# Seven products for eight in the head projections of a two-layer MLA and short-convolution trunk

## The chip, the cores and the metric

The kernel runs on one core of a Trainium2 chip. The metric is the device time of the program in microseconds (us). TensorE is PE in the profile (PEld is its weight load), VectorE is DVE, ScalarE is ACT, GpSimd is POOL and SyncE is SP.

## The reference

Two request groups share the weights: 512 prompt tokens and 64 sample tokens that attend to 512 cached ones. All is float32. Each of two layers computes

```
h = rmsnorm(x);  z = h @ w_in
b, c, xin, cq, ckv, kpe, ga, gb = split(z)         # 1024,1024,1024,384,256,64,1024,1024
y_a = b * causal_conv3(c * xin)
q = rmsnorm(cq) @ w_uq;  rotary parts turned       # 8 heads, 128 + 64
k = ckv_n @ w_uk;  v = ckv_n @ w_uv                # ckv_n = rmsnorm(ckv)
y_b = softmax(q k^T masked by chunks of 64) v
x += rmsnorm((sigmoid(ga) * y_a + sigmoid(gb) * y_b) @ w_o)
x += rmsnorm(relu(rmsnorm(x) @ w1)^2 @ w2)
```

The outputs are x, the new latents, rotated keys and convolution states. The gates, b, c and xin of head h are the columns 128h to 128h+127 of their parts of w_in: five blocks of 1024x128 for each head.

## The kernel before

**Layout.** Features lie on the partitions, the 576 tokens on the free axis, in two halves of 288. A float32 product is made of three fp32r matmuls (`mm3`): weight low part by x high part, high by low, high by high. So each weight block of 128x1024 (512 KB) is loaded raw into one of eight slots by SyncE, copied to a high part by ScalarE (`w_hi`) and subtracted to a low part by VectorE (`w_lo`).

**A head.** TensorE's program is written out by hand. For each of eight heads: block 0 (gate gb), the projections (an even head also makes the rotary queries of two heads and the values of two heads), block 1 (gate ga), absorbed sample queries and scores, block 2 (c), turns (transposes) of the probabilities, block 3 (xin), the attention product, block 4 (b). A block is two halves of 24 matmuls of 128x288 into a ring of four PSUM banks (`ring_free`, `ring_full`), from which VectorE scales it by the row norm `rx`. Between scores and turns stand VectorE's row maxima (L2159 to L2166), ScalarE's four exponents (L1348) and VectorE's scaling of the probabilities (L2184). `normed` releases the turns. `pv_read` says that the attention product was read from PSUM; the next head's keys wait for it.

**Loads.** SyncE loads a head's block into the slot whose block was just used (L846, after `ring_full`), five blocks ahead. In each head, after `absorbed`, it loads the small projection weights of the next one (`small_raw`). All its DMAs are on one queue, q1.

**Sums of weights.** The feed-forward's first matrix is already used in couples: 2x2 quarters with seven products instead of eight (`pair`), whose four weight sums GpSimd makes in DRAM by nine accumulating or plain DMAs each (`weight_sums`, L974 to L986, queue q0), 12 couples in each layer, after the two halves of the key's rotation (`key_rope`, L999 to L1008) of that layer.

**Start of layer 1.** SyncE waits for `row_sum`, loads the cosine and sine tables (L820, L821), then weights of head 0 (L768). ScalarE converts the second of them (L1034) in front of the key's last half.

Of the kernel before, what the change touches and what calls it, by code (L numbers as in the profile page):

```python
# [84 lines left out]
def use_hd(h, i):  # L85
    return h + (2 if SLOT_HD[i] in SLOT_P1 else 1)


def use_wo(m):
    return use_hd(HEADS, m) if m < N_HEAD else 2  # L90


def ffn_loads():
# [18 lines left out]
    uses = {SLOT_WO[m]: use_wo(m) for m in range(8)}  # L112
    use_of = {}
# [7 lines left out]
    return use_of, [uses[s] for s in range(8)]  # L121


USE_OF, SLOT_USES = ffn_loads()


# [16 lines left out]
def summed_no(L, g, p):  # L143
    return 16 * (pair_no(L, g, p) + 1)


# [3 lines left out]
R3 = HD0 + 10 * HEADS  # L150
# [14 lines left out]
def r_hd(e, i, s):  # L165
    return HD0 + 10 * e + 2 * i + s
# [130 lines left out]
class Plan:  # L297


    def __init__(self, nc, ctx):  # L300
        self.nc = nc
        self.memory()
        self.sums = nc.dram_tensor("weight_sums", (DEPTH * PAIRS, P, 4, 512), F32, kind="Internal").ap()
# [129 lines left out]
        self.left_copied = semaphore("left_copied")  # L433
        self.right_copied = semaphore("right_copied")
        self.left_added = semaphore("left_added")
        self.sum1_made = semaphore("sum1_made")
        self.sum2_made = semaphore("sum2_made")
        self.sum4_made = semaphore("sum4_made")
# [14 lines left out]
    def memory(self):  # L453
# [21 lines left out]

        self.x = put("x", [P, KC, NT])
# [7 lines left out]
        self.xh, self.xl = split("xs", [P, KC, NT])  # L484
        self.my = put("my", [P, KC, NT])
# [31 lines left out]
        self.probs = put("probs", [P, PCOLS])  # L517
        self.pth, self.ptl = split("probs_t", [P, PCOLS])
# [3 lines left out]
        turn = mark[0]  # L522
        self.cv = put("cv", [P, NT + 2])
        self.u = put("u", [P, NT + 4])
        after_head, mark[0] = mark[0], turn
        self.rope_t, self.rope_s = put("rope_t", [P, 2, NH]), put("rope_s", [P, 2, NH])
        assert mark[0] <= after_head
# [51 lines left out]
        tile, row = 4 * 4 * NH, 4 * NH  # L579
        hi_at = [small_at, small_at + 2 * tile, p1 + tile, sums]  # L580
# [123 lines left out]
def lo_made(L, n):  # L704
    return L * NBC + n + 1
# [56 lines left out]
def loads(nc, block, pl, x_in, consts, tables, blocks, small, uv, cache_t, cache_n, cache_pe, x_out):  # L762
# [3 lines left out]
    def _(sp):  # L766
# [39 lines left out]
        for L in range(DEPTH):  # L806
# [12 lines left out]
            sp.wait_ge(pl.row_sum, 2 * L + 1)  # L819
            sp.dma_start(pl.cos[:, :], tables[0]).then_inc(pl.tables_landed, 16)  # L820
# [4 lines left out]
            for p in range(HEADS // 2):  # L825
                for e in range(2):
                    for i in range(N_HEAD):
                        if i == 2:

                            sp.wait_ge(pl.absorbed, L * HEADS + p * 2 + (e + 1))  # L830
                            if e == 0:
                                odd_small(L, p)
                            elif p < HEADS // 2 - 1:
                                even_small(L, p + 1)
                            else:
                                sp.dma_start(pl.sraw[:, 0:SMV], small[L * 5 + HEADS // 2][:, 0:SMV]) \
                                    .then_inc(pl.small_landed, 16)
                        if p * 2 + e == HEADS - 1 and i == 2:
                            sp.dma_start(pl.ctraw[:, :, 0:PAST], cache_t[L]).then_inc(pl.cache_landed, 16)
                            for rows in (slice(0, ROPE), slice(ROPE, P)):  # L840
                                sp.dma_start(pl.kcraw[rows, 0:PAST], cache_pe[L]).then_inc(pl.cache_landed, 16)
                            sp.wait_ge(pl.scored, (L + 1) * HEADS * KT)
                            sp.dma_start(pl.naraw[:, :, :], cache_n[L]).then_inc(pl.nat_landed, 16)
                        sp.wait_ge(pl.ring_full, p * 20 + full(L, r_hd(e, i, 1)))

                        sp.dma_start(pl.slot(SLOT_HD[i])[2], blocks[L * NB + p * 10 + (n_head(e + 1, i))]) \  # L846
                            .then_inc(pl.slots[SLOT_HD[i]], 16)
# [23 lines left out]
            def pair_load(g, p, i):  # L871
                s = slots_pair(g, p)[i]
                to = pl.slot(s)[2]
                if i == 0:
                    slot_load(L, n_w1(g, 2 * p), s)
                elif i == 1:
                    sp.dma_start(to[:, 512:1024], blocks[L * NB + n_w1(g, 2 * p + 1)][:, 512:1024]) \
                        .then_inc(pl.slots[s], 16)
                else:
                    if i == 2:  # L880
                        sp.wait_ge(pl.sum2_made, summed_no(L, g, p))
                    else:
                        sp.wait_ge(pl.sum1_made, summed_no(L, g, p))
                        sp.wait_ge(pl.sum4_made, summed_no(L, g, p))
                    sp.dma_start(to.rearrange("p (b k) -> p b k", b=2),
                                 pl.sums[pair_no(L, g, p)][:, 2 * i - 4:2 * i - 2, :]).then_inc(pl.slots[s], 16)
# [75 lines left out]
def rotation_and_sums(nc, block, pl, blocks):  # L962
# [3 lines left out]
    def _(pool):  # L966

        def weight_sums(L, g, p):

            made, done = pl.sums[pair_no(L, g, p)], summed_no(L, g, p)  # L970
            a11, a12 = (blocks[L * NB + n_w1(g, 2 * p)][:, 512 * k:512 * (k + 1)] for k in range(2))
            a21, a22 = (blocks[L * NB + n_w1(g, 2 * p + 1)][:, 512 * k:512 * (k + 1)] for k in range(2))
            sum2, sum3, sum1, sum4 = (made[:, k, :] for k in range(4))
            pool.dma_start(sum2, a11).then_inc(pl.left_copied, 16)  # L974
            pool.dma_start(sum3, a11).then_inc(pl.left_copied, 16)
            pool.dma_start(sum1, a22).then_inc(pl.right_copied, 16)
            pool.dma_start(sum4, a12).then_inc(pl.right_copied, 16)
            pool.wait_ge(pl.left_copied, 2 * done)
            pool.dma_start(sum3, a21, accum_op=ALU.add).then_inc(pl.left_added, 16)
            pool.dma_start(sum2, a21, accum_op=ALU.add).then_inc(pl.left_added, 16)  # L980
            pool.wait_ge(pl.right_copied, 2 * done)
            pool.dma_start(sum1, a21, accum_op=ALU.add).then_inc(pl.sum1_made, 16)
            pool.wait_ge(pl.left_added, 2 * done)
            pool.dma_start(sum2, a22, accum_op=ALU.add).then_inc(pl.sum2_made, 16)
            pool.wait_ge(pl.sum2_made, done)
            pool.dma_start(sum4, sum2, accum_op=ALU.add).then_inc(pl.sum4_made, 16)  # L986
# [24 lines left out]
        for L in range(DEPTH):  # L1011
# [12 lines left out]
def scalar_engine(nc, block, pl, x_in, x_out, kv_out, kpe_out, conv_out):  # L1024
# [4 lines left out]
    def _(eng):  # L1029
# [8 lines left out]

        def head_hi(L, i):
            weight_hi(L, n_head(0, i), SLOT_HD[i], use_hd(0, i))  # L1040
# [105 lines left out]
        for L in range(DEPTH):  # L1146
# [109 lines left out]
            for p in range(HEADS // 2):  # L1256
                for e in range(2):
                    def of_head(per_head, j):
                        return L * (HEADS * per_head) + p * (2 * per_head) + (e * per_head + j + 1)
# [532 lines left out]
def vector_engine(nc, block, pl):  # L1792
# [4 lines left out]
    def _(eng):  # L1797
# [9 lines left out]
        def p1_lo(L, b):  # L1807
            weight_lo(L, b, SLOT_P1[b])
# [1559 lines left out]
```

## Time and profile before

| | |
|---|---|
| median of 3 runs | 1749.77 us (1749.56 to 1752.14) |
| the profiled execution | 1752.92 us, its span 1751.1 us |
| busy share of the span | PE 99%, PEld 98%, DVE 66%, ACT 45%, POOL 10% |
| DMA queue of SyncE, q1 | 163.82 MB |
| DMA queue of GpSimd, q0 | 56.64 MB |

The profile page divides the span into 40 slices; each digit is the busy share of a slice in tenths, and PEclk is the granted clock of TensorE in the same way. Matmuls are pipelined, so the start of one to the start of the next is their cost, not their duration. A window's row gives its length, then each engine's busy time with instruction counts, the granted clock, the mean busy share of the 16 DMA engines and their GB/s.

### The profile page before, as it was taken

The numbers are of one execution on the slowest core, as the hardware profiler recorded it, in microseconds if no ns is written. First come the engines' busy times: TensorE is split into PE (matmuls) and PEld (weight loads), VectorE is DVE, ScalarE is ACT, GpSimd is POOL, SyncE is SP. The second block draws the span as 40 slices with busy tenths as digits, with TensorE's granted clock in tenths as the row PEclk, the third lists the DMA queues.
The fourth block names the chain that finished last, engine by engine and source line by source line (L and its number), as shares of the span: only waits on it lengthen the run. The fifth ranks groups of instructions, "written<-read, shape, count | busy, mean of one in ns | idle before, by whom it ended". The sixth has DMA issues, their size and how long they took to land.

```text
span 1751.1 us, 31636 instructions
## 1 busy us (share of the span) xinstructions
PE 1736.5 (99%) x12975; PEld 1723.4 (98%) x12975; DVE 1156.4 (66%) x2232; ACT 794.3 (45%) x1541; POOL 167.9 (10%) x239
## 2 busy tenths in 40 slices
PE   9999999999999999999999999999999999999998
PEld 9999999999999999999999999999999999999997
DVE  7765555658798566657687555556577886666565
ACT  7634343335465454435366343434345545444452
POOL 0322222000000000000003222222000000000000
PEclk9999999999999999999999999999999999999999
DMA  4688878432213434333227887887513214333331
GB/s 175 174 197 178 192 176 186 106 100 76 86 52 110 131 123 133 121 116 132 74 95 157 168 159 176 148 176 155 135 62 109 74 67 164 120 116 119 126 110 55
DMA packets 83904, 224.57 MB, mean 128 GB/s; under 512 B 9776, under 2 KB 21296, under 8 KB 83760
## 3 DMA queue, kind: packets, MB, share of 16 engines
q1 hardware_dynamic: 57520, 163.82, 28.5%
q0 software_dynamic: 24960, 56.64, 19.3%
q8 instruction: 103, 1.69, 0.4%
q10 hardware_dynamic: 1280, 2.10, 0.4%
q14 instruction: 41, 0.34, 0.1%
HBM read 218.65 MB, written 60.49 MB: 159 GB/s over the span
## 4 chain that ended last, share of the span: by engine, by line
PE 97%; DMA 2%; DVE 1%; ACT 0%; SPq 0%; issue 0%; DVEq 0%
PE ring L720 20%; PE ring L722 20%; PE ring L721 20%; PE att L720 11%; PE att L722 11%; PE att L721 11%; PE att L2992 1%; DMA w_raw<-blocks_in 1%; DMA small_raw<-small_in 1%; PE att L715 1%; PE att L714 1%; PE att L727 0%; PE att L728 0%; PE att L2807 0%; PE att L3048 0%; DVE last L2761 0%
## 5 line engine op out<-in xcount | busy, mean ns | idle before, releaser
L720 PE MATMUL ring<-xs_hi,w_lo 128*128 128x288 f32 x2272 | 674.9, 297 | 0.9 <-issue 0.4
L722 PE MATMUL ring<-xs_hi,w_hi 128*128 128x288 f32 x2272 | 669.2, 295 | 0.0
L721 PE MATMUL ring<-xs_lo,w_hi 128*128 128x288 f32 x2272 | 669.0, 294 | 0.0
L720 PEld LDWEIGHTS ring<-xs_hi,w_lo 128*128 128x128 f32 x2272 | 426.7, 188 | 3.3 <-issue 0.8
L721 PEld LDWEIGHTS ring<-xs_lo,w_hi 128*128 128x128 f32 x2272 | 426.9, 188 | 1.6
L722 PEld LDWEIGHTS ring<-xs_hi,w_hi 128*128 128x128 f32 x2272 | 426.6, 188 | 0.0
L1800 DVE TENSOR_TENSOR w_lo<-w_raw,w_hi 128x1024 fp32r<-128x1024 f32 (+1 forms) x286 | 330.5, 1167 | 73.3 <-ACT w_hi L1270 60.5
L722 PE MATMUL att<-f_hi,w_hi 128*128 128x288 f32 x960 | 283.2, 295 | 0.0
L721 PE MATMUL att<-f_lo,w_hi 128*128 128x288 f32 x960 | 282.9, 295 | 0.0
L720 PE MATMUL att<-f_hi,w_lo 128*128 128x288 f32 x960 | 282.6, 294 | 0.0
L721 PEld LDWEIGHTS att<-f_lo,w_hi 128*128 128x128 f32 x960 | 180.4, 188 | 0.0
L720 PEld LDWEIGHTS att<-f_hi,w_lo 128*128 128x128 f32 x960 | 180.4, 188 | 0.0
L722 PEld LDWEIGHTS att<-f_hi,w_hi 128*128 128x128 f32 x960 | 180.4, 188 | 0.0
L1034 ACT ACTIVATE w_hi<-w_raw 128x1024 fp32r<-128x1024 f32 x106 | 109.7, 1053 | 96.9 <-DMA w_raw<-blocks_in 96.9
L2429 DVE TENSOR_TENSOR my<-att,my 128x288 f32<-128x288 f32 x160 | 73.2, 457 | 113.2 <-PE att L722 113.0
L720 PE MATMUL ring<-mix_hi,w_lo 128*128 128x288 f32 x384 | 113.4, 295 | 0.0
L722 PE MATMUL ring<-mix_hi,w_hi 128*128 128x288 f32 x384 | 113.2, 295 | 0.0
L721 PE MATMUL ring<-mix_lo,w_hi 128*128 128x288 f32 x360 | 106.2, 295 | 0.0
L1270 ACT ACTIVATE w_hi<-w_raw 128x1024 fp32r<-128x1024 f32 x80 | 84.0, 1052 | 43.4 <-DMA w_raw<-blocks_in 43.4
L1547 ACT ACTIVATE ft<-ft 128x288 f32<-128x288 f32 x96 | 42.2, 440 | 70.5 <-DVE ft L2537 35.7
L722 PEld LDWEIGHTS ring<-mix_hi,w_hi 128*128 128x128 f32 x384 | 72.3, 188 | 0.0
L720 PEld LDWEIGHTS ring<-mix_hi,w_lo 128*128 128x128 f32 x384 | 72.1, 188 | 0.0
(297 smaller groups left out, 2727.9 us busy)
## 6 DMA issues: line engine op xcount, KB each, us to landing
w_raw<-blocks_in SPq DMA_DIRECT2D x211, 512.0 KB, 4.3
weight_sums<-blocks_in POOLq DMA_DIRECT2D x192, 256.0 KB, 6.8
w_raw<-weight_sums SPq DMA_DIRECT2D x48, 512.0 KB, 3.8
w_raw<-blocks_in SPq DMA_DIRECT2D x26, 256.0 KB, 3.3
weight_sums<-weight_sums POOLq DMA_DIRECT2D x24, 256.0 KB, 6.3
small_raw<-small_in SPq DMA_DIRECT2D x16, 320.0 KB, 4.7
small_raw<-small_in SPq DMA_DIRECT2D x32, 128.0 KB, 5.9
x<-x_in SPq DMA_DIRECT2D x8, 288.0 KB, 6.8
```

The costliest lines, as they stand in the source:

```text
L714: pe.matmul(out, both, keys[1], start=False, stop=False)
L715: return pe.matmul(out, both, keys[0], start=False, stop=True)
L720: pe.matmul(out, w[1], x[0], start=first, stop=False)
L721: pe.matmul(out, w[0], x[1], start=False, stop=False)
L722: return pe.matmul(out, w[0], x[0], start=False, stop=last)
L1034: act.activation(hi, raw, ACT.Copy).then_inc(pl.weights_hi, 1)
L1270: act.activation(hi, raw, ACT.Copy).then_inc(pl.weights_hi, 1)
L1547: act.activation(ft, ft, ACT.Relu).then_inc(pl.pair_relu, 1)
L1800: return dve.tensor_tensor(out, a, hi.bitcast(F32), ALU.subtract)
L2429: dve.tensor_tensor(dst, src, dst, ALU.add).then_inc(pl.w2_free, 1)
L2992: last = pe.transpose(att[:, to:to + P], pl.probs[:, PO[t] + P * j:PO[t] + P * (j + 1)], ident)
```

## The change

Heads 2 to 6 are "mixed". Each has two couples. A couple takes two blocks of weights, A = (a11, a12) and B = (b21, b22) in quarters of 512 rows, and the two halves of tokens and of features of the normed x, and makes four results by seven products of 12 matmuls instead of eight. The first couple is c with xin (blocks 2 and 3), the second gb with ga (blocks 0 and 1); block 4 (b) stays plain. The order on TensorE in a mixed head is

```
projections, 7 products, absorbed queries and scores, block of b, turns, 3 products, attention product, 4 products
```

so there is no block in front of the projections any more. Each mixed head uses eight slots of loads instead of five (raw halves and sums), so that 55 positions in place of 40 pass the five head slots of a layer.

**Activations.** The products need the normed x itself and four mixtures of its quarters. VectorE writes x times gain times rx over x in head 0 (three rows before the row maxima, five at the end); SyncE stores it (`h_kept`) and loads it back at the end of head 1 into the low part; in head 1 VectorE makes the four mixtures (`head_mix`, 128x1152 each, two of them in front of the row maxima), ScalarE their high and VectorE their low parts, two before the attention output and two behind the merge; the normed x's parts follow in head 2. The mixtures lie where x and my lay. So each head's row of my is stored to DRAM after its merge, and at the start of head 7 SyncE stores the last row, waits for it, and loads seven rows of my and all of x (from `x_in` or `x_kept`) in front of the weights of position 55 on; in layer 1 x is first stored to `x_kept` in front of the tables.

**Sums.** GpSimd makes the sums of 22 couples per layer, 44 in all, in one run in layer 0 after the key's rotation, and only then comes to layer 1's rotation. Eight DMAs' worth of data each (one copy writes two sums), in batches: copies of sum n+1, first adds of n, second of n-1, third of n-2, after waiting for all of the batch before.

**Results.** ScalarE keeps product 0 (`snapshot`), VectorE combines the others in seven small steps per couple; since the x used is normed, the multiplications by rx fall away. In a mixed head the convolution's first tap on ScalarE comes before the exponents, VectorE's two taps between the row maxima and the probabilities, and the attention output comes after the last product and its gate. The low parts of positions at+4 to at+6 are made between the steps of the first couple.

The core of the diff:

```diff
+FIRST_MIXED, LAST_MIXED = 2, 6
...
+            def product(h, c, i):
+                n, idx = 9 * c + i, r_mixed(h, 9 * c + i)
+                eng.wait_ge(pl.ring_free, may_fill(L, idx))
+                if n % 2 == 0:
+                    eng.wait_ge(pl.weights_lo, pos_made(L, HEAD_POS[h] + n // 2))
...
+                x_of = (normed(0, 0), normed(4, 0), turned(1), turned(2), turned(3), turned(0), normed(4, 1))[i]
+                half_product(idx, half_weight(h, n), x_of, True, True).then_inc(pl.ring_full, 1)
...
+            def mixed_head(h):
+                projections(h)
+                for i in range(7):
+                    product(h, 0, i)
+                scores(h)
+                mixed_block(h)
+                turns(h)
+                for i in range(3):
+                    product(h, 1, i)
+                attended(h)
+                for i in range(3, 7):
+                    product(h, 1, i)
```

SyncE, in the loop over the heads:

```diff
+            if L > 0:
+                sp.wait_ge(pl.x_new, x_new(L - 1, "post_b", KC - 1))
+                sp.dma_start(pl.x_kept, pl.x[:, :, :]).then_inc(pl.x_spilled, 16)
             sp.dma_start(pl.cos[:, :], tables[0]).then_inc(pl.tables_landed, 16)
...
+            for h in range(HEADS):
+                if h > 0:
+                    sp.wait_ge(pl.merged, L * HEADS + h)
+                    sp.dma_start(pl.my_kept[:, h - 1, :], my_row(pl, h - 1)).then_inc(pl.my_stored, 16)
+                if h == 1:
+                    sp.wait_ge(pl.h_made, KC * (L + 1))
+                    sp.dma_start(pl.h_kept, pl.x[:, :, :]).then_inc(pl.h_stored, 16)
+                if h == HEADS - 1:
+                    sp.wait_ge(pl.my_stored, stored(L, HEADS - 2))
+                    sp.dma_start(pl.my[:, 0:KC - 1, :], pl.my_kept[:, 0:KC - 1, :]).then_inc(pl.my_landed, 16)
+                    sp.dma_start(pl.x[:, :, :], x_in if L == 0 else pl.x_kept).then_inc(pl.x_back, 16)
+                for j in range(HEAD_POS[h + 1] - HEAD_POS[h]):
...
+                    elif is_mixed(h):
+                        sp.wait_ge(pl.ring_full, full(L, r_mixed(h, (1, 3, 5, 8, 9, 11, 13, 15)[j])))
+                    else:
+                        sp.wait_ge(pl.ring_full, full(L, r_hd(h, j, 1)))
+                    pos_load(HEAD_POS[h] + j + N_HEAD)
```

GpSimd, and VectorE's order in head 1 and in a mixed head:

```diff
+            for n in range(n_sums + 2):
+                if n < n_sums:
+                    pool.wait_ge(pl.sums_copied, 48 * (n + 1))
+                if 1 <= n <= n_sums:
+                    pool.wait_ge(pl.sums_first, 32 * n)
+                if 2 <= n <= n_sums + 1:
+                    pool.wait_ge(pl.sums_second, 16 * (n - 1))
+                if n >= 3:
+                    pool.wait_ge(pl.sums_third, 16 * (n - 2))
+                if n + 1 < n_sums:
+                    sums_copy(n + 1)
+                if n < n_sums:
+                    sums_add_first(n)
+                if 1 <= n <= n_sums:
+                    sums_add_second(n - 1)
+                if n >= 2:
+                    sums_add_third(n - 2)
...
-            for g in range(FIRST_PAIR, GROUPS):
-                for p in range(2):
-                    weight_sums(L, g, p)
+            if L == 0:
+                all_sums()
...
+                elif h == FIRST_MIXED - 1:
+                    head_mix(0)
+                    head_mix(1)
+
+                row_maxima(h)
...
+                pos_lo(L, at + 6)
+                lower_right(0, pl.v2[:, :])
+                upper_right(0, pl.cv[:, cols(1)])
+                conv_second_half()
+
+                row_maxima(h)
+                absorbed_lo(h, pl.rest)
+                conv_taps(h)
+                probabilities(h)
```

## Rows read from the trace of the kernel before

**Rows 1.** Page: busy time, and granted clock in 40 slices.
```profile
PE 1736.5 (99%) x12975; PEld 1723.4 (98%) x12975; DVE 1156.4 (66%) x2232; ACT 794.3 (45%) x1541; POOL 167.9 (10%) x239
...
PEclk9999999999999999999999999999999999999999
```

**Rows 2.** TensorE's waits: us in total, times, longest.
```profile
PE att L720 <- DVE ckv_lo L1800: 2.4, 1, 2.4
...
PE att L720 <- DVE probs_t_lo L1800: 1.1, 1, 1.1
```

**Rows 3.** Windows by stage, head 2 of layer 0; DMA share last but one.
```profile
148.04:157.08 9.04, 9.04 (x68) 8.77 (x67) 5.29 (x12) 6.86 (x16) 2.77 (x4) 1.00 0.92 212
157.08:163.44 6.36, 6.36 (x51) 6.36 (x49) 4.02 (x8) 2.34 (x5) 0.83 (x1) 1.00 0.70 97
163.44:167.07 3.63, 3.63 (x27) 3.41 (x26) 1.73 (x3) 1.80 (x3) 0.26 (x1) 1.00 0.93 128
...
180.88:182.74 1.86, 1.86 (x15) 1.73 (x13) 0.64 (x3) 1.02 (x3) 0.00 (x0) 1.00 1.12 184
```

**Rows 4.** Timeline of VectorE in the same head: start, us, instruction.
```profile
151.24 0.46 DVE L2125 TENSOR_TENSOR rope_t<-att,cos 128x288 f32<-128x288 f32 x1 [5.71 <-ACT rope_s L1108]
...
152.10 0.46 DVE L2128 TENSOR_TENSOR rope_t<-rope_t,rope_s 128x288 f32<-128x288 f32 x1
...
165.80 1.23 DVE L1800 TENSOR_TENSOR w_lo<-w_raw,w_hi 128x1024 fp32r<-128x1024 f32 x1 [1.70 <-ACT w_hi L1270]
...
169.38 0.29 DVE L2174 TENSOR_TENSOR q_abs_lo<-att,u 128x128 fp32r<-128x128 f32 x1
...
171.94 1.27 DVE L2184 TENSOR_SCALAR probs<-probs,ri 128x128 f32<-128x128 f32 x4
...
188.15 0.19 DVE L2235 TENSOR_SCALAR gate_sample<-gb 128x64 f32<-128x64 f32 x1
188.25 0.68 DVE L2237 SCALAR_TENSOR_TENSOR my<-gb,att 128x512 f32<-128x512 f32 x1
...
189.89 0.69 DVE L2092 TENSOR_TENSOR my<-my,ga 128x512 f32<-128x512 f32 x1
```

**Rows 5.** DMA view: queue's packets, MB, share; issues with us to landing.
```profile
q1 hardware_dynamic: 57520, 163.82, 28.5%
...
w_raw<-blocks_in SPq DMA_DIRECT2D x26, 256.0 KB, 3.3
...
x_out<-x ACTq DMA_DIRECT2D x2, 288.0 KB, 2.3
```

**Rows 6.** Loads of w_raw, from 100 to 320 us and from 340 to 440 us.
```profile
DMA to landing us min/median/max: 3.5/5.6/7.6
...
DMA to landing us min/median/max: 3.4/3.7/5.3
```

**Rows 7.** Queues in windows 59:66, 277:300 (two), 613:700, 1189.5:1216 us.
```profile
q0 software_dynamic: 304, 1.00, 47.3%
...
q0 software_dynamic: 1040, 2.36, 58.2%
q1 hardware_dynamic: 457, 1.62, 23.7%
...
q1 hardware_dynamic: 3302, 11.00, 38.6%
...
q0 software_dynamic: 1040, 2.36, 60.4%
```

**Rows 8.** Chain that ended last, at the start of layer 1.
```profile
908.91 8.76 DMA w_raw<-blocks_in
...
917.70 1.06 ACT w_hi L1034
```

**Rows 9.** Timeline of GpSimd: first sum of layer 0, rotation of layer 1.
```profile
59.66 0.71 POOL L974 DMA_DIRECT2D weight_sums<-blocks_in  x1
...
913.76 0.79 POOL L999 TENSOR_TENSOR rope_t<-kpe,cos 128x288 f32<-128x288 f32 x1 [592.87 <-DMA sin<-tables_in]
```

More of the change, by code:

```diff
@@ L110, in ffn_loads @@
     order += [("w2", g, j) for g, j in W2_LAST]
-    uses = {SLOT_WO[m]: use_wo(m) for m in range(8)}
-    use_of = {}
+    uses, use_of = [int(s in SLOT_P1) for s in range(8)], {}
+    for q in range(POSITIONS + N_HEAD):
+        two = any(is_mixed(h) and HEAD_POS[h] + 2 <= q < HEAD_POS[h] + 7 for h in range(HEADS))
+        uses[pos_slot(q)] += 2 if two else 1
+        use_of["pos", q] = uses[pos_slot(q)]
+    for m in range(N_HEAD, 8):
+        uses[SLOT_WO[m]] += 1
+        use_of["wo", m] = uses[SLOT_WO[m]]
     for block in order:
@@ L824, in _ @@
                 slot_load(L, n_head(0, i), SLOT_HD[i])
[L825 to L847, printed above, removed]
@@ L966, in _ @@
     def _(pool):
[L968 to L986, printed above, removed]
@@ new lines, in rotary_lo @@
+            def rotary_lo(h):
+                for half in range(2):
+                    cs = cols(half)
+                    eng.wait_ge(pl.rope_hi, h + (L * 8 + half + 1))
+                    for rows, other, both in ((slice(0, ROPE), slice(ROPE, P), pl.pe0),
+                                              (slice(ROPE, P), slice(0, ROPE), pl.pe1)):
+                        ins = minus(both[other, cs], pl.rope_t[rows, half, :], both[rows, cs])
+                    ins.then_inc(pl.rope_lo, 1)
@@ new lines, in keys, with values @@
+            def keys(h):
+                eng.wait_ge(pl.pv_read, of_head(h, 1, 0))
+                for c in range(CC):
+                    last = mm3(pe, att[:, 1024:1536], small_w(SK, c), rows_of(ckv, ALL, c, slice(0, NP_)),
+                               c == 0, c == CC - 1)
+                last.then_inc(pl.projected, 1)
+            def values(two):
+                tiles = value_tiles(pl, two)
+                for kt in range(2):
+                    at = P * (2 * two + kt)
+                    for c in range(CC):
+                        last = mm3(pe, tiles[:, kt, :, :], rows_of(ckv, ALL, c, slice(at, at + P)),
+                                   rows_of(small, ALL, slice(SV + 2 * P * c, SV + 2 * P * (c + 1))),
+                                   c == 0, c == CC - 1)
+                last.then_inc(pl.projected, 1)
@@ new lines, in turns @@
+            def turns(h):
+                eng.wait_ge(pl.normed, of_head(h, 4, KT - 1))
+                eng.wait_ge(pl.abs_lo, of_head(h, 1, 0))
+                for j, at in enumerate((1536, 0, 512, 768)):
+                    for t in range(j, KT):
+                        to = at + P * (t - j)
+                        last = pe.transpose(att[:, to:to + P], pl.probs[:, PO[t] + P * j:PO[t] + P * (j + 1)], ident)
+                    if j != 2:
+                        last.then_inc(pl.turned, 1)
@@ new lines, in half_weight, with half_product @@
+            def half_weight(h, n):
+                hi, lo, _ = pl.half_slot(pos_slot(HEAD_POS[h] + n // 2), n % 2)
+                return hi, lo
+            def half_product(idx, weight, x_of, first, last):
+                for k in range(4):
+                    w = slice(k * P, (k + 1) * P)
+                    ins = mm3(pe, pl.ring[:, bank(L, idx), 0:NH], (weight[0][:, w], weight[1][:, w]), x_of(k),
+                              first and k == 0, last and k == 3)
+                return ins
```

1141 lines of the change are left out of this document (758 added, 383 removed).

## Prediction

> **What bounds the kernel now.** I read the busy row and the forty slices first [rows 1]: TensorE is busy 99% of the span, at full clock in every slice, while VectorE stands at 66% and ScalarE at 45%. Then TensorE's waits [rows 2]: 2.4 us for ckv_lo in layer 1, 1.1 for a low part of the turned probabilities, and no longer one in the heads. So every matmul left out gains its pitch, and every wait on TensorE's way is new time. The stages of head 2 in layer 0 [rows 3] give all lengths: projections of an even head 9.04 us, a block of 48 matmuls 6.36 (0.1325 each), absorbed queries and scores 3.63, attention product 1.86. The last column but one matters as much: the DMA engines stand at 0.70 to 1.12 there, because GpSimd's queue makes the weight sums.
>
> **The gain.** Before, a head has five blocks, 240 matmuls. After, a mixed head has two couples of seven products of 12 and one block: 168 + 48 = 216. 24 x 0.1325 = 3.18 us, in 5 heads of 2 layers: **31.8 us** off. All matmuls kept have their old shapes.
>
> **Layer-wide costs, each on the path.** Times below count from T, the start of the head in question on TensorE.
> (a) Head 1. VectorE now makes two mixes of 128x1152 before its row maxima. A 128x1024 difference takes 1.23 us [rows 4], so two take some 2.6 with the wait between them. Before, VectorE finishes w_lo at 167.03 and the scores end at 167.07; from there maxima, exponents and probabilities last until 173.21, and the block that covers them until 167.07 + 6.36 = 173.43 [rows 3, 4]: no slack. Cost 2.6 us per layer.
> (b) Head 2's start. It has no block 0 in front any more (6.36 us of cover). At the end of head 2 the attention output began at 188.15 and the merge ended at 190.58 [rows 4], with the next head at 182.74 + 6.36 = 189.10 [rows 3]. In head 1 one low weight of 1.2 goes away in front of it and two low parts of mixes come, 1.3 each: merge at T+2.9; two more behind it: T+5.5. The first rotary sum takes 1.3 us [rows 4], T+6.8, and TensorE wants it at T+5.2 (18 matmuls of queries 2.4; of the 4.3 us left of 9.04 for keys and values, by columns 1.4 each for keys and half the values). Then a normed low part stands before the low keys (0.8 us more), another before product 1 (0.4), and VectorE reaches the row maxima 0.8 late. About 3.7 us per layer.
> (c) Heads 3 to 6. The keys want pv_read, which now comes after the last product: with 0.3 until the last product can be read, 0.46 combination, 0.69 and 0.2 gate and 0.78 attention output (widths as in [rows 4]) TensorE has it at T+2.5 against T+2.4. About 0.2 each, 0.8 per layer.
> (d) The slot at+6 is loaded when product 3 is done, 4.8 us before the scores. Two halves of 256 KB land 3.3 us after the second issue [rows 5], at -0.6; ScalarE 1.05, VectorE 1.2 [rows 4, 8], then lower right 0.95, upper right 0.45, convolution input 0.5: +3.6, and the scores end at +3.63. Borderline: 0 to 0.5, I take 0.2 a head, 1.0 per layer.
> (e) Head 7. SyncE waits for the merge of head 6 (T+3.3), stores its row (288 KB, 2.3 us by the nearest store [rows 5]), and issues at T+6 the rows kept, 2.06 MB, and x, 2.36 MB. Behind them on the same queue comes the weight for position 55, 0.52 MB, which ScalarE converts before the absorbed queries and VectorE before the row maxima. The queue needs 28.5% of 1751 us for 163.8 MB [rows 5], 3.05 us per MB: 4.94 MB land at T+6.3+15.1+1.5 = T+22.9; +1.05+1.2 = T+25.1. The scores end at T+20.1 (6.36+3.78+6.36+3.63). The row maxima start 5.0 us late, per layer. Bounds: 0, if a load doesn't wait for larger ones in front of it, and 20, below.
> [...] The queue's own row gives 328 GB/s over the span, so I keep 3.05 us per MB.
> (f) Layer 1 only: x, 2.36 MB, is stored in front of the tables and of three weights of head 0. The second of these landed 8.76 us after 908.91; ScalarE, which has key and latent work behind it, started it at 917.70; this ended in the 2.4 us wait [rows 2, 8]. With 2.36 x 3.05 = 7.2 us more in front, the wait grows by 7.1. Nothing covers it; bounds 0 and 14 (a queue shared with the sums).
> Sum: layer 0 13.1, layer 1 20.2 us. Other new loads, the extra ScalarE copies and the 1.68 us of taps lie in idle time: the two taps, some 1.7 us by the 128x512 line, fit the time from 169.67 to 171.94 in which VectorE waited for exponents [rows 4].
>
> **Costs of a full DMA in layer 0.** GpSimd now makes all 44 sums in one run from about 60 us on [rows 9], batch behind batch, instead of 12 in each layer. So all heads and the feed-forward of layer 0 run beside them. Before, the same contention made a weight load land in 5.6 us (median, up to 7.6) against 3.7 in the quiet stretch [rows 6], without a wait on TensorE. Now (d) has no slack: 1.8 us in each of five heads, 9 us. The slot at+10, loaded 8.2 us before the head's end, delays lower right and with it pv_read: 1.2 us in four heads, 5 us. (e) has 15.1 us of transfer that shares its engines; at the factor that 5.6 against 3.7 gives on 1.6 us of transfer (2.2, less for pauses between batches: 1.6) it is 24, +9 us. Sum **23 us**; bounds 0 and 45. The feed-forward's loads land several us before VectorE's turn, so I charge nothing there; if that cover were gone, each pair would cost a us or two.
>
> **Does GpSimd finish in time?** Its next duty is layer 1's key rotation, at 913.76 before [rows 9]. A sum's nine DMAs took 58.2% of 23 us, 13.4 us of all engines, the four copies 3.3 of it (47.3% of 7 us) [rows 7]; now four copies and four adds, about 11. With 3 us for issue and receipt between batches and SyncE's queue taking 0.24 to 0.39 of the engines [rows 7], a batch takes 17 to 21 us; 45 of them end between 825 and 1005. The share of 1.12 in [rows 3] says that the queues overlap a little, so I take 19.3: 930. The need moves to 913.8 + 7 (f) + 20 (layer 0) = 941. Just in time: charge 0, with the overrun as a rival.
>
> **Sum.** -31.8 + 13.1 + 20.2 + 23 = +24.5 us on the profiled execution, whose own time is 1752.92 (span 1751.1); that one stands 3.15 us above the median of the runs. So 1749.8 + 24.5 = **1774 us**.
>
> **Rivals.**
> Rival 1, GpSimd is late. In layer 1 a sum needed 60.4% of 26.5 us, 16 us instead of 13.4 [rows 7]; if the sums of layer 1 are as dear when made early, batches take 22 us after the first 22 and the run ends near 1000. Layer 1's rotation then waits 40 to 60 us, TensorE with it: about 1820. For it: those rows. Against: before, latency filled much of each chain. It begins where a batch takes over 19.6 us.
> Rival 2, the queues share without harm: layer 0 costs what layer 1 does, no 23 us. -31.8 + 33.3 = +1.5, 1751. For it: sums before cost TensorE nothing. Against: the slack that made this so is what the change uses up.
> Rival 3, the other side: loads behind a large transfer aren't held up, since sixteen engines take both in turn. Then (e) and (f) fall away and contention too: -31.8 + 16.2 = -15.6, 1734. It decides if position 55 lands by T+18. Against it: the weight of 8.76 us in [rows 8], which had only 1.6 MB in front.
> [...]
>
> **Chances and range.** Forecast 0.40, rival 1 0.25, rival 2 0.15, rival 3 0.20. Half of rival 3 lies under 1733 and the far part of rival 1 over 1830, so the range is 1733 to 1830; the forecast's own is 1760 to 1795. A change under 0.2% (3.5 us) can't be told from none. Faster: rival 3 and a part of rival 2, 0.22; same 0.07; slower 0.71.
>
> **What would show it.** Right: TensorE waits before turns in heads 1 and 7 of both layers, about 2.6 and 5 us (14 in layer 0); a wait of some 9 us near layer 1's start with a weight load behind it; landings of 6 us or more in layer 0 up to its end, under 4 in layer 1's heads; 12735 matmuls. Wrong: position 55 lands within 12 us of T+6; GpSimd's DMAs end before 800 (they were cheap in batches) or after 950 (rival 1), then with a wait on kpe in layer 1; or TensorE's waits sum to under 30 us. A lower granted clock behind the longer waits would add to all of this.

## The result and the profile after

The changed kernel takes 1911.44 us (median of 4 runs, 1904.33 to 1916.63) against 1749.66 (1749.02 to 1752.14): a ratio of 1.0919, 95% interval 1.0881 to 1.0957. The forecast was 1774 us, its range 1733 to 1830. The page of its profiled execution, in answer to [rows 1] (busy time, then three of the lines in 40 slices):

```profile
span 1907.8 us, 31819 instructions
...
PE 1730.6 (91%) x12735; PEld 1711.7 (90%) x12735; DVE 1254.1 (66%) x2370; ACT 855.2 (45%) x1617; POOL 245.8 (13%) x331
...
PE   9989899989999999999940099999999999999998
...
PEclk9989999999999999999975599999999999999999
DMA  5698889897777988997876433433361222433331
```

The 240 matmuls less are there and TensorE's busy time is 6 us shorter, but it stands still in slices 21 to 23. Its waits, in answer to [rows 2]:

```profile
PE att L797 <- DVE rope_t L2369: 109.3, 3, 106.0
PE att L3456 <- DVE probs L2409: 36.4, 9, 12.2
PE att L797 <- DVE ckv_lo L2051: 12.2, 2, 11.6
```

One wait of 106.0 us is in layer 1's start; the second row is turns in the heads that wait for VectorE's probabilities. The chain of what ended last runs through GpSimd's queue: "issue" (time in which an engine stood and the profile shows nothing that it waited for) has 30.0% of the span there and DMAs of weight_sums 13.2%. The next rows are the timeline of GpSimd, to be read beside [rows 9], at its last sum, and that of TensorE behind it (start, duration; in brackets the idle time before and what ended it):

```profile
1085.42 0.81 POOL L1129 DMA_DIRECT2D weight_sums<-weight_sums  x1 [5.09 <-DMA weight_sums<-weight_sums]
1085.97 1.08 POOL L1164 TENSOR_TENSOR rope_t<-kpe,cos 128x288 f32<-128x288 f32 x1
...
1093.64 0.61 PE L797 MATMUL att<-cqn_hi,small_lo 128*128 128x288 f32 x1 [106.04 <-DVE rope_t L2369]
```

The rotation of layer 1 starts right behind the issue of the last sum, at 1085.97 instead of 913.76 [rows 9]. The first rotary sum of head 0 on VectorE stands behind the key in program order, so the wait shows under its name. Where the time went, by the start of the turns of head 0 and head 7 in each layer (taken at their first weight load):

| stretch | before | after | difference |
|---|---|---|---|
| start to turns of head 0, layer 0 | 83.6 | 83.7 | +0.1 |
| to turns of head 7, layer 0 | 311.3 | 349.0 | +37.7 |
| to turns of head 0, layer 1 | 555.0 | 681.7 | +126.7 |
| to turns of head 7, layer 1 | 312.7 | 305.0 | -7.7 |
| to the end | 488.5 | 488.4 | -0.1 |

The rows of the windows (length, busy times, granted clock, DMA share, GB/s) say what stood beside each stretch:

```profile
60.00:440.00 380.00, 341.31 (x2390) 333.37 (x2390) 256.53 (x509) 167.97 (x310) 85.48 (x116) 0.94 0.86 211
440.00:900.00 460.00, 456.60 (x3444) 456.02 (x3443) 311.07 (x573) 214.70 (x402) 100.83 (x136) 1.00 0.83 192
...
972.00:1083.00 111.00, 6.53 (x30) 5.78 (x30) 6.12 (x10) 6.47 (x15) 26.61 (x35) 0.53 0.61 97
1130.00:1450.00 320.00, 313.92 (x2293) 307.47 (x2292) 242.16 (x487) 157.29 (x292) 0.00 (x0) 0.99 0.44 143
```

Heads with sums beside them (first row) lose 39 of 380 us and some of the clock. Heads without (last row) run nearly full and are faster than before. And the 37.7 us of layer 0 are not even part of the end: the rotation waited for GpSimd, whose run of sums began at the same 60 us as before, so without the 37.7 us TensorE would only have stood longer. On the path stand 172.2 us of rotation later, less 7.7 between rotation and first turns (28.4 for 36.1 us; I take it that TensorE had by then done all that needs no key), less 7.7 in layer 1's heads: 156.8, the difference of the two spans (156.7).

Why was GpSimd late? Its 44 sums took from 60 to 1086, 22.4 us each from the last add of the first (122.1) to that of the last (1085.4). One batch, while the feed-forward ran:

```profile
613.65 0.77 POOL L1116 DMA_DIRECT2D weight_sums<-blocks_in  x1 [5.12 <-DMA weight_sums<-weight_sums]
614.40 0.57 POOL L1117 DMA_DIRECT2D weight_sums<-blocks_in  x1
614.94 0.55 POOL L1118 DMA_DIRECT2D weight_sums<-blocks_in  x1
615.47 0.93 POOL L1122 DMA_DIRECT2D weight_sums<-blocks_in  x1
623.13 0.84 POOL L1123 DMA_DIRECT2D weight_sums<-blocks_in  x1 [6.74 <-issue]
623.68 1.13 POOL L1126 DMA_DIRECT2D weight_sums<-weight_sums  x1
632.06 0.81 POOL L1129 DMA_DIRECT2D weight_sums<-weight_sums  x1 [7.26 <-issue]
637.96 0.76 POOL L1116 DMA_DIRECT2D weight_sums<-blocks_in  x1 [5.09 <-DMA weight_sums<-weight_sums]
```

The program waits only in front of L1116. Yet GpSimd stands before L1123 and L1129, each time 7 us, and the trace has no semaphore for it ("issue"). The view of GpSimd's waits counts them over the whole span:

```profile
POOL weight_sums L1123 <- issue: 273.3, 42, 14.5
POOL weight_sums L1129 <- issue: 261.2, 42, 8.8
```

535 us of standing that the prediction's batch did not have.

### The profile page after: what moved, and what is told of

Read it like the earlier page. It is cut to its first block, busy times and chain, and to the rows that moved or that the text cites. A ratio compares the mean times of both kernels' runs of the same rounds, so it can differ in the third digit from the quotient of the medians.

```text
span 1907.8 us, 31819 instructions
## 1 busy us (share of the span) xinstructions
PE 1730.6 (91%) x12735; PEld 1711.7 (90%) x12735; DVE 1254.1 (66%) x2370; ACT 855.2 (45%) x1617; POOL 245.8 (13%) x331
## 3 DMA queue, kind: packets, MB, share of 16 engines
q1 hardware_dynamic: 76288, 204.32, 32.8%
q0 software_dynamic: 38720, 92.29, 27.4%
q10 hardware_dynamic: 1280, 2.10, 0.3%
## 4 chain that ended last, share of the span: by engine, by line
PE 40%; issue 30%; DMA 16%; POOL 10%; DVE 3%; ACT 1%; SPq 0%; POOLq 0%; DVEq 0%; ACTq 0%
DMA weight_sums<-weight_sums 13%; PE ring L797 8%; PE ring L799 8%; PE ring L798 8%; PE att L797 5%; PE att L799 5%; PE att L798 5%; POOL weight_sums L1122 2%; POOL weight_sums L1126 2%; POOL weight_sums L1123 2%; POOL weight_sums L1116 2%; POOL weight_sums L1117 1%; DMA w_raw<-blocks_in 1%; POOL weight_sums L1118 1%; DMA weight_sums<-blocks_in 1%
## 5 line engine op out<-in xcount | busy, mean ns | idle before, releaser
L797 PE MATMUL ring<-xs_hi,w_lo 128*128 128x288 f32 x1872 | 561.0, 300 | 1.6 <-ACT kpe L1341 0.5
L798 PE MATMUL ring<-xs_lo,w_hi 128*128 128x288 f32 x1872 | 555.0, 296 | 0.0
L799 PE MATMUL ring<-xs_hi,w_hi 128*128 128x288 f32 x1872 | 554.5, 296 | 0.0
L2051 DVE TENSOR_TENSOR w_lo<-w_raw,w_hi 128x1024 fp32r<-128x1024 f32 (+1 forms) x316 | 367.7, 1171 | 119.7 <-ACT w_hi L1206 82.9
L797 PEld LDWEIGHTS ring<-xs_hi,w_lo 128*128 128x128 f32 x1872 | 355.9, 190 | 4.4 <-issue 1.3
L798 PEld LDWEIGHTS ring<-xs_lo,w_hi 128*128 128x128 f32 x1872 | 355.7, 190 | 1.6
L799 PEld LDWEIGHTS ring<-xs_hi,w_hi 128*128 128x128 f32 x1872 | 355.2, 190 | 0.0
L1206 ACT ACTIVATE w_hi<-w_raw 128x1024 fp32r<-128x1024 f32 x118 | 124.4, 1056 | 168.9 <-DMA w_raw<-weight_sums 85.8
L1198 ACT ACTIVATE w_hi<-w_raw 128x1024 fp32r<-128x1024 f32 x98 | 102.3, 1056 | 109.8 <-DMA w_raw<-blocks_in 109.8
L797 PE MATMUL att<-cqn_hi,small_lo 128*128 128x288 f32 x144 | 43.5, 302 | 106.3 <-DVE rope_t L2369 106.0
L797 PEld LDWEIGHTS att<-cqn_hi,small_lo 128*128 128x128 f32 x144 | 28.0, 195 | 106.7 <-DVE rope_t L2369 106.2
```

Of the source, the lines that this page charges most:

```text
L797: pe.matmul(out, w[1], x[0], start=first, stop=False)
L798: pe.matmul(out, w[0], x[1], start=False, stop=False)
L799: return pe.matmul(out, w[0], x[0], start=False, stop=last)
L1198: act.activation(hi, raw, ACT.Copy).then_inc(pl.weights_hi, 1)
L1206: act.activation(hi, raw, ACT.Copy).then_inc(pl.weights_hi, 1)
L2051: return dve.tensor_tensor(out, a, hi.bitcast(F32), ALU.subtract)
```

## The experiments

Times of before, measured beside the runs: 1750.25 us for runs 1, 2, 3 and 5, 1749.55 for 6, 7, 9 and 10, 1750.63 for 4, 8 and 11. L0 and L1 below are the stretches from turns of head 0 to turns of head 7 in the two layers.

**1. Sums of each layer in that layer.**

```diff
-            if L == 0:
-                all_sums()
+            layer_sums(L)     # 22 sums, same batches
```

> All 44 sums are still made in batches, but the 22 of layer 1 only after layer 1's key rotation. Theory 'GpSimd is late' (the rotation queued behind 44 batches costs the 106 us stop of TensorE in layer 1 and a few us of half clock behind it): the stop falls away, some 1911 - 108 = 1803 us if layer 1's heads stay as fast as they are, and up to 45 us more, 1848, if sums beside the heads cost in layer 1 what they cost in layer 0 (turns of head 0 to turns of head 7: 349 us against 305). Rival (the stop has another cause, the stored x or the tables): still a stop of 100 us, 1900 or more.

1832.71 us (1829.39 to 1851.78), ratio 1.0494 (1.044 to 1.0549). The stop is gone: the rotation starts at 950.35, and TensorE's longest wait for a rotary sum is 2.2 us. L0 is 343.0 and L1 351.7, where it was 305.0. So the late rotation is the cause of the stop, and sums beside mixed heads cost layer 1 some 47 us too.

**2 and 3. GpSimd's DMA scratch and its use.** In the first, one number of the program's set-up, the size of its DMA scratch; in the second, one issue. I expected 1820 to 1870 us of both and 19 to 22 us a sum. "Descriptor space", here and in run 4, is only my name for the scratch: no trace shows what it holds, and that GpSimd stands because it is full is my inference.

```diff
-    nc = bacc.Bacc(..., dynamic_dma_scratch_size=1024)
+    nc = bacc.Bacc(..., dynamic_dma_scratch_size=1280)
```

> [...] Rival (the DMA engines themselves are the limit, at a share of 0.83): batches and time unchanged, 1905 to 1915.

```diff
-            pool.dma_start(pl.sums[n][:, 2, :], b[:, 512:1024], accum_op=ALU.add)...
-            pool.dma_start(pl.sums[n][:, 1, :], b[:, 0:512], accum_op=ALU.add)...
+            pool.dma_start(pl.sums[n][:, 1:3, :], b.rearrange("p (k c) -> p k c", k=2), accum_op=ALU.add)...
```

> The two first adds of a sum, 256 KB each, are one DMA of 512 KB: the same bytes, one issue less. [...] Rival (bytes through the engines): batch 23.3 us, time 1905 to 1915.

1823.88 us (1.0424, 1.0408 to 1.0439) and 1810.46 us (1.0325, 1.0286 to 1.0364). The sums end at 930.8 and 927.5 us, 19.1 and 19.0 us each; the rotations, at 987.96 and 978.03, wait for the sine table and no longer for GpSimd. (Run 3 came out faster than the 1820 that I expected at the least.) The timeline of GpSimd with 1280 bytes:

```profile
605.13 0.76 POOL L1116 DMA_DIRECT2D weight_sums<-blocks_in  x1 [10.43 <-DMA weight_sums<-weight_sums]
605.88 0.57 POOL L1117 DMA_DIRECT2D weight_sums<-blocks_in  x1
606.41 0.55 POOL L1118 DMA_DIRECT2D weight_sums<-blocks_in  x1
606.94 0.91 POOL L1122 DMA_DIRECT2D weight_sums<-blocks_in  x1
607.49 1.21 POOL L1123 DMA_DIRECT2D weight_sums<-blocks_in  x1
614.93 0.81 POOL L1126 DMA_DIRECT2D weight_sums<-weight_sums  x1 [6.23 <-issue]
615.46 1.14 POOL L1129 DMA_DIRECT2D weight_sums<-weight_sums  x1
```

One stop instead of two, and one DMA later (in front of L1126 instead of L1123), as I had expected; the bytes of both queues are unchanged (92.29 and 204.32 MB). The stop that is left is not small: in all sums together GpSimd still stands 245 us in run 2 and 286 in run 3, against 535. And the time is not 1774: L0 is 367.9 and 360.4, longer than the 349.0 of the change, and the stretch between the layers' heads is 573.8 and 569.2 where it was 555.0 before. I put this down to the faster queue: from 84 to 433 us the DMA engines' share is 0.93 and 0.89, against 0.88 in the change.

**4. Half the space.** Same line, 512.

> The changed kernel with 512 bytes of descriptor scratch instead of 1024, nothing else. Theory 'descriptor space' (1024 bytes held five units of 128 rows, 1280 held six): two units fit, so GpSimd stands at up to four DMAs of a batch instead of two, a batch takes 30 us or more instead of 22.4, the rotation comes at 1350 or later and the time is over 2150 us. Rival (stops come from the engines' share): 1911 us as before.

2301.55 us (2296.74 to 2306.36; 1.3149). Sums take 30.9 us each, the rotation starts at 1473.28, TensorE waits 404.9 us for it. A batch:

```profile
618.42 0.76 POOL L1116 DMA_DIRECT2D weight_sums<-blocks_in  x1 [5.73 <-DMA weight_sums<-weight_sums]
619.17 0.57 POOL L1117 DMA_DIRECT2D weight_sums<-blocks_in  x1
624.32 0.55 POOL L1118 DMA_DIRECT2D weight_sums<-blocks_in  x1 [4.57 <-issue]
624.85 0.90 POOL L1122 DMA_DIRECT2D weight_sums<-blocks_in  x1
629.64 0.85 POOL L1123 DMA_DIRECT2D weight_sums<-blocks_in  x1 [3.90 <-issue]
634.43 0.82 POOL L1126 DMA_DIRECT2D weight_sums<-weight_sums  x1 [3.94 <-issue]
```

So 30.9, 22.4 and 19.1 us for 512, 1024 and 1280 bytes, with the same DMAs. The five and six units that I had in mind are what GpSimd issued in front of its first stop in the change (L1116, two units of 128 rows, to L1122) and in run 2 (to L1123); here it issued three (L1116 and L1117), where I expected two. While it ran, the engines' share between 600 and 700 us was 0.66 against 0.85 in the change: they had more room, and GpSimd did not fill it.

**5. No sums.** Every read of a sum by SyncE reads a plain block:

```diff
-                return pl.sums[head_sums(L, h, c)][:, k, :]
+                return half_of(h, 3 * c % 4, k % 2)
...
-            if L == 0:
-                all_sums()
```

> Leaves out all weight sums: GpSimd issues no DMA, and SyncE loads plain weights of the same size in their place. Every other instruction stays. It gives the price of the change without GpSimd's queue. Prediction's terms without contention: 1749.8 - 31.8 + 33.3 = 1751 us. By the turns measured in layer 1 (heads 7.9 us shorter than before, its sums were all done): heads of both layers give 16 us, layer 1's start costs 9, so 1743 us. Rival (heads of layer 0 are slow for a reason other than the sums, such as the 2.36 MB store in front of a weight of head 1): layer 0 still costs 10 to 30 us more than layer 1, 1755 to 1775.

1743.47 us (1739.61 to 1744.93), ratio 0.9959 (0.9944 to 0.9973). L0 303.9, between 559.5, L1 304.6. This is the change without GpSimd's queue, to be held against the prediction without its 23 us (1751). Waits of TensorE, then what follows the longest wait of the turns (layer 1, head 1):

```profile
PE att L3429 <- DVE probs L2382: 8.6, 5, 2.4
PE att L797 <- DVE ckv_lo L2024: 4.8, 2, 4.4
```

```profile
992.65 2.22 PE L3429 MATMUL att<-consts,probs 128*128 128x128 f32 x10 [2.36 <-DVE probs L2382]
...
994.90 0.44 PE L798 MATMUL ring<-xs_lo,w_hi 128*128 128x288 f32 x1
995.14 0.44 PE L799 MATMUL ring<-xs_hi,w_hi 128*128 128x288 f32 x1
...
996.33 0.30 PE L798 MATMUL ring<-xs_lo,w_hi 128*128 128x288 f32 x1
996.46 0.29 PE L799 MATMUL ring<-xs_hi,w_hi 128*128 128x288 f32 x1
```

After a wait of 2.4 us the matmuls start 0.24 us apart until 996.1, then 0.13. The granted clock is 0.50 from 994.5 to 996.0 and 1.00 from 996.5 on. That adds nearly 2 us to the wait.

**6. No sums, four steps elsewhere.**

```diff
-            if L > 0: ... sp.dma_start(pl.x_kept, pl.x[:, :, :])          # ahead of tables
+            ...                                                         # behind head 0's weights
-                if h == 1: ... sp.dma_start(pl.h_kept, pl.x[:, :, :])
-                if h == HEADS - 1: ... my_kept -> my, x_in or x_kept -> x
                     pos_load(HEAD_POS[h] + j + N_HEAD)
+                    if h == 1 and j == 2: ...
+                    if h == HEADS - 1 and j == 1: ...
-                    head_mix(0); head_mix(1)                             # ahead of row_maxima
+                    # 0 behind absorbed_lo, 1 behind next_weight(2), 2 and 3 behind the first product with cv
```

> As the run without sums (weight sums left out, plain weights of the same size loaded instead), with four steps put elsewhere. SyncE stores x in layer 1 behind the three weights of head 0, stores the normed x in head 1 behind three weight loads, and loads my and x in head 7 behind positions 54 and 55; VectorE makes the mixes of head 1 behind the row maxima (first), behind w_lo (second) and inside block 3's work (third and fourth). Theory 'these places are what layer costs without contention': against 1743.5 us the wait for ckv_lo (4.4) falls to about 0, the waits before the turns of head 1 (2.6 in each layer) and head 7 (1.8 and 2.2) go, and with them 1 to 2 us of half clock behind each, together 14 to 22 us: 1722 to 1730. Rival (the work only moves on to the next reader, above all the turned probabilities and head 2's start): new waits of the same size there, 1738 to 1748.

1741.1 us (1740.58 to 1743.13; 0.9951, 0.9936 to 0.9966), 2.4 us less than run 5, whose own times lie between 1739.61 and 1744.93: no gain that can be told from none. Turns of heads 1 and 7 no longer wait, L0 is 299.8 and L1 300.5, about 4 us less each. But the waits of TensorE now begin

```profile
PE ring L797 <- DVE xs_lo L2688: 5.1, 2, 3.2
PE att L797 <- DVE rope_t L2342: 4.4, 2, 2.2
PE att L797 <- DVE probs_t_lo L2024: 3.5, 2, 2.5
```

The merged rows' low parts (my came back later), head 2's rotary sum and the turned probabilities take what the turns gave: the rival, that the wait only moves on to the next reader.

**7. Sums in three parts.** Merged adds, and

```diff
             if L == 0:
-                all_sums()
+                sums_of(0, 10)
+                pool.wait_ge(pl.merged, HEADS)
+                sums_of(10, 32)
+            else:
+                pool.wait_ge(pl.merged, 2 * HEADS)
+                sums_of(32, 44)
```

> All 44 sums, first adds merged as before in one DMA, but in three parts: 10 head sums of layer 0, then from the end of layer 0's heads its 12 couples of the feed-forward and the 10 head sums of layer 1, then from the end of layer 1's heads its 12 couples. The 22 sums of the middle part take 22 x 19 = 418 us from about 440 on and end near 860, ahead of the rotation's need at about 960. Theory 'heads of a layer pay only for DMAs beside them': layer 0's heads 2 to 6 pay until the tenth sum is done (near 270 us), heads 5 to 7 then run as in the kernel without sums, so the 49 us that this layer's heads lost fall to 25 to 35; layer 1 as before; start of layer 1 5 us instead of 14: 1810 - 15 to 25 - 9 = 1776 to 1786 us. Rival (the first couples of the feed-forward now come late): a wait of 10 us or more on a weight in the feed-forward of layer 0 or 1, 1800 us or more.

1782.66 us (1780.06 to 1791.63; 1.0195, 1.0167 to 1.0223). L0 335.5, between 561.1, L1 305.8. The tenth sum has landed by 269. Windows on either side of it, for this run and for the change:

```profile
100.00:275.00 175.00, 147.59 (x1016) 143.79 (x1015) 115.20 (x216) 73.74 (x132) 33.79 (x45) 0.92 0.84 208
275.00:430.00 155.00, 152.82 (x1124) 149.92 (x1123) 111.50 (x232) 72.87 (x136) 0.00 (x0) 1.00 0.48 154
```

```profile
100.00:275.00 175.00, 156.75 (x1089) 152.99 (x1089) 119.60 (x228) 75.24 (x134) 37.59 (x51) 0.93 0.87 207
275.00:430.00 155.00, 137.85 (x969) 134.39 (x967) 96.43 (x202) 61.88 (x116) 34.60 (x47) 0.94 0.89 229
```

Once the queue is silent TensorE is busy 152.8 of 155 us at full clock, where the change had 137.9: heads pay only for DMAs beside them. The expected rival, a wait of 10 us or more in the feed-forward, did not come.

**8. Plain DMAs for the accumulating ones**, in run 7's order.

> The run in three parts (1782.7 us) with plain DMAs of the same shape and waits in place of the accumulating ones, so the adding is left out and the sums are not sums. [...] Rival (any second queue beside the loads costs the same): heads and time as before, 1780 to 1785.

1757.44 us (1753.91 to 1760.88; 1.0041, 1.0028 to 1.0053); L0 318.9. Half of L0's excess over run 5 went (335.5, 318.9, 303.9), and the time fell below the 1762 that I expected. Ten sums took GpSimd until 217 us instead of 269. Windows of run 8 on either side of that point and, below, of run 7:

```profile
100.00:212.00 112.00, 98.14 (x678) 94.98 (x678) 78.61 (x143) 48.76 (x85) 22.64 (x41) 0.94 0.86 266
212.00:268.00 56.00, 55.21 (x411) 54.37 (x410) 42.09 (x85) 26.93 (x51) 0.52 (x1) 1.00 0.45 133
```

```profile
100.00:212.00 112.00, 98.00 (x676) 95.60 (x675) 78.51 (x143) 47.88 (x84) 23.79 (x33) 0.94 0.88 232
212.00:268.00 56.00, 42.59 (x289) 41.19 (x288) 32.33 (x68) 21.81 (x40) 10.00 (x13) 0.88 0.86 184
```

While both queues ran, TensorE was busy the same 98 of 112 us: the engines were as full (0.86 and 0.88), although w_raw landed in 5.5 us (median) instead of 8.2 (3.2 without any sums, by run 5). The gain came behind 212 us, 55.2 of 56 us against 42.6, because the plain queue was done. While it ran, the queue's share did not fall to the 35 to 40% that I expected (46.1% against 50.3% from 100 to 212 us), and the heads beside it ran no faster; a plain sum is only done sooner. From 110 to 270 us GpSimd's queue took 50.0% of sixteen engines for 14.96 MB with adds and 29.4% for 14.42 MB without.

**9 to 11. Mends on run 7**: the large transfers behind the weights; that and the mixes; and a milder form of both.

> As the run in three parts, with SyncE's three large transfers (x to DRAM at layer 1's start, the normed x to DRAM in head 1, my and x back in head 7) put behind the weight loads that stood behind them. Theory 'a weight queued behind a large transfer is late': the weight of head 1 no longer lands 16 us after its issue, the wait before head 1's turns falls from 6 to 3 us, that before head 7's from 7 or more to under 3, the one at layer 1's start from 4.6 to about 0: 12 to 20 us less than the run in three parts. Rival (the engines' share is what delays them, not the place in the queue): under 4 us less.

> The run before with VectorE's mixes of head 1 behind the row maxima too: all mends together, a full version of the kernel. By the sums: 31.8 us less of matmuls, heads of layer 0 dearer by 10 to 25 us for the sums beside them, 8 us for head 2's start in both layers: 1750 - 31.8 + 18 to 33 = 1736 to 1751 us. Theory 'the change pays once its DMAs are off the path': under 1746. Rival (contention in layer 0's heads 2 to 5 eats the gain): 1755 to 1775.

> The run in three parts with four places changed, each once: x to DRAM in layer 1 behind the weights, the normed x to DRAM behind two loads, mixes of head 1 behind the row maxima, and in head 7 my brought back first as in the change but x behind positions 54 and 55. Theory 'only x was too much in front of position 55': no wait before the turns of heads 1 and 7 and no low parts late behind them (5.1 us in the run without sums), 1770 to 1778 us. Rival (whatever is taken from one wait comes back at the next reader on the same engine): 1780 to 1792.

1785.61 us (1.0188, 1.0162 to 1.0214), 1791.2 (1.024, 1.0197 to 1.0284) and 1786.63 (1.0222, 1.0188 to 1.0257). None is better than run 7, from which run 9 (1777.56 to 1791.37) can't be told. L0 fell a little (331.1, 335.1, 331.4), but the stretch between rose (573.8, 577.4, 563.0 against 561.1), in run 9 with waits for low parts of the turned probabilities (3.1 us) and merged rows (1.5) and one of 4.2 us that the trace calls issue. These stretches overstate the difference: the profiled executions of runs 9 and 10 were their slowest (1791.37 and 1801.02), that of run 7 its fastest (1780.06). Waits in the stretch, from 415 to 1000 us, sum to 14.1 us in run 9 against 8.0 in run 7; where the rest of the 12 us went was not followed further. My theories failed here; of the rivals only that of run 11 (1780 to 1792) came true.

## Why the prediction was wrong, point by point

**The step that failed** is "Does GpSimd finish in time?". It priced a batch as engine time of its eight DMAs plus 3 us of latency, all in flight together, took 19.3 us, and let the run end at 930, just before the need at 941. The 3 us were an estimate of mine, which no row shows; in the change GpSimd stood 5.6 us on average in front of a batch until the last add had landed (229.0 us in 41 waits). In the kernel as it is, GpSimd issued a batch in three goes, with 6.7 and 7.3 us of standing between them in the batch above, and a sum took 22.4. The run ended at 1085, 155 us late; 3.1 us in each of 44 sums are 136 of them, and this moved the rotation past its need. With a scratch of 1280 bytes, or one issue less, a sum takes 19.0 to 19.1 us and the run ends at 927.5 to 930.8, as forecast. But this does not confirm the term: in those runs too GpSimd stood once in each batch, and accumulating batches all in flight were never run, so their price stays open and the match with 19.3 is in part luck. Rival 1 had the place, the wait and its threshold of 19.6 us, but for another reason (dearer sums of layer 1), gave 1820, and got 0.25.

The trace of before could have spoken: its GpSimd waited for a landing between its DMAs, with five in flight at most, so no row showed what happens with more. A limit that no row shows should have widened the batch upwards; its bounds were put at 17 to 21 by the engines alone. The runs showed one: with 512, 1024 and 1280 bytes of scratch (run 4, the change, run 2) a sum takes 30.9, 22.4 and 19.1 us.

**Costs of a full DMA in layer 0**: forecast 23 us (bounds 0 and 45), measured 45.1 (349.0 against 303.9 without sums). 32 of them are waits (38.4 us between 60 and 450 against 6.1); the other 13 go with the lower clock behind them (the granted clock is 0.94 there against 1.00). This term failed too, and by itself it would have spoilt the forecast: in run 3, where GpSimd is in time, the profiled span is 63.3 us over that of run 5, 56.5 of it in L0 and 9.6 in the stretch between. Two parts were missed. In head 1 the normed x, 2.36 MB, is stored in front of a weight:

```profile
105.57 0.33 SPq L960 DMA_DIRECT2D h_kept<-x  x1
106.12 0.33 SPq L845 DMA_DIRECT2D w_raw<-blocks_in  x1
...
122.79 1.06 ACT L1206 ACTIVATE w_hi<-w_raw 128x1024 fp32r<-128x1024 f32 x1 [5.33 <-DMA w_raw<-blocks_in]
...
134.01 2.39 PE L3456 MATMUL att<-consts,probs 128*128 128x128 f32 x10 [7.80 <-DVE probs L2409]
```

That weight came 16.7 us after its issue, its low part stood in front of the mixes and maxima, and the turns waited 7.8 us instead of 2.6. And the prediction said that a lower clock "would add" and gave it no term. In the feed-forward nothing was charged, and waits there came to 3.9 us. The sign that it named, landings of 6 us or more, did not show: w_raw's median from 84 to 433 us was 5.2.

**The gain**, 31.8: right. From turns of head 2 to those of head 6 the kernel without sums takes 166.7 us, before 179.3: 12.6 less, by the prediction 4 x 3.18 = 12.7.

**The layer-wide costs**, measured without sums (run 5) unless said otherwise:

- **(a)** Forecast 2.6 us per layer. The wait is 2.4 in both layers, and nearly 2 of half clock come behind it.
- **(b)** Forecast 3.7. From turns of head 1 to those of head 2 it is 49.9 us, in layer 0 as in layer 1. Before it was 47.5, with 240 matmuls of blocks; now there are 144 of blocks and 84 of products, 12 fewer, 1.6 us: 45.9. Of the 4.0 more, 1.2 is the wait for the rotary sum, 0.6 other waits and about 2 the clock behind (a). With the mixes moved (run 6) it was 50.3, so this start is dear by itself.
- **(c) and (d)** Forecast 1.8 together. Measured 0.1, in the same 12.6.
- **(e)** Forecast 5.0 per layer. From turns of head 6 to those of head 7 it was 42.2 us before; also 12 matmuls fewer now, so 40.6; measured 42.4 and 43.0, 1.8 and 2.4 more. The rate was right: in layer 1 of the change my was issued at 1395.89, position 55 at 1397.44, and it landed 13.4 us later, 4.94 MB in 15.0 us, 3.03 us per MB. But the queue began with my 1.5 us before the point from which I counted, and I had added a latency of 1.5 on top: 13.4 us from there instead of 16.6. With sums beside it in layer 0 of the change it took 20 us for the same, and the turns waited 12.2 (forecast 14).
- **(f)** Forecast 7.1. The wait grew from 2.4 to 4.4, and the stretch between the layers by 4.5. In run 6 that wait is down to 1.0, yet the stretch is 560.1: the other waits there took its place.

Sum of layer costs: forecast 33.3, measured 24 (31.8 less the 8.0 us by which the span of run 5 is shorter).

**Rival 2** (the queues share without harm, 1751) is refuted by the 45.1 us; its time is near that of run 5, 1743, only because there is no second queue in it. **Rival 3** is refuted: loads do stand behind large ones, at 3.03 us per MB. With position 55 put ahead of them in both layers its waits went away, and with the weight of layer 1 put ahead all but 1.0 us of its wait (run 6).

## What to carry to other kernels

When GpSimd's DMAs are batched, count what may be in flight and not only bytes: look for "issue" between two of its DMAs with no wait in the program, and if it is there, enlarge the scratch or merge DMAs. Here they took 88 and 101 us off (runs 2 and 3). Ask of any long background run which later duty stands behind it on the same engine, and split the run there. And a background queue that cost nothing while loads had slack is no longer free once a change uses up that slack: here the sums alone turned -0.4% into +2% at the best order found.

## What the runs showed of the hardware that I had not expected

- **GpSimd stood earlier in a batch with accumulating DMAs than with plain ones**, as if they took twice the scratch: an estimate of mine from where it stood. In front of L1126 it stood 38 times in run 7, 254.0 us in all, and 3 times, 15.7 us, with plain ones in run 8. Count a plain DMA of 128 rows as one and an accumulating one as two; the first copy of a sum (L1116), which writes two quarters, has 256 rows and counts as two. Issued without a stop at 1024 bytes: 6 (change, two more did not fit), 7 with plain DMAs (run 8, batches in steady state); at 1280 bytes: 8 (two more did not fit); at 512 bytes: 3 (one more did not). A merged add with rows of 4 KB counts as one of 2 KB. All fit a scratch of 7 to 8 counts at 1024 bytes, in proportion at the others; the counts within a DMA were not measured by themselves. My expectations had said five and six equal units, which run 8 contradicts. One thing the count leaves open: at the start of each of its three parts run 8 stands at L1118 and then at L1126 (5.5 and 6.1 us in the first part), with three and five counts issued since the last wait.
- **An accumulating DMA costs more of the engines**: 50.0% against 29.4% of sixteen engines for nearly the same 15 MB. While both queues ran, though, the heads lost the same with either: TensorE was busy 98 of 112 us (runs 7 and 8).
- **Two short waits cost clock.** Behind waits of 2.4 us (run 5) and 7.8 us (the change, head 1) the granted clock was 0.50 for 3.5 and 5 us; by half of these times it cost about 2 us on top each time. A lower clock (0.94 against 1.00) goes with 13 of the 45 us that layer 0's heads lost.
